# A state-space scan that steps over pairs of time steps, with its lookup tables built as products of two small ones

## The reference, cut to what matters

```
mag = exp(a_re * dt); lb = mag * (cos(a_im * dt) + i sin(a_im * dt))
bb = coef * b                                 # per group 64 x 16, complex
bu[l, g, p] = sum_c u[l, g, c] * bb[g, p, c]
x[l] = lb * x[l-1] + bu[l]                    # along all 512 tokens
y[l, g, c] = Re(sum_p c[g, c, p] * x[l, g, p]) + d_skip[g, c] * u[l, g, c]
s = gelu(y); s = s * sigmoid(s @ w_glu + b_glu)
y_b = (s * silu(ssm_gate)) @ w_ssm_out
```

## Time and profile before

| | |
|---|---|
| time, median of 3 runs (lowest, highest) | 1187.76 us (1187.38, 1188.01) |
| the profiled execution: its own time | 1186.81 us |
| the profiled execution: span, first to last instruction | 1185.0 us |
| mean granted clock of PE, of full speed | 0.998 |
| busy: PE, weight loads of PE, DVE, ACT, POOL | 1158.0, 949.8, 752.5, 403.4, 11.8 us |

### The profile page before, as it was taken

How to read it: one execution, slowest core, us unless ns; L and a number is a source line. 1 busy time by engine, 2 the same in 40 slices (tenths; PEclk the granted TensorE clock), 3 DMA queues, 4 the chain that set the end, 5 groups by cost and what they waited for, 6 DMA issues and landing times.

```text
span 1185.0 us, 13271 instructions
## 1 busy us (share of the span) xinstructions
PE 1158.0 (98%) x5357; PEld 949.8 (80%) x5357; DVE 752.5 (64%) x1317; ACT 403.4 (34%) x526; POOL 11.8 (1%) x12
## 2 busy tenths in 40 slices
PE   5999999999999999999999999999999999999997
PEld 4999888888777788887777777788888888887886
DVE  5887568999777778628999999443133343423324
ACT  7423243332376543332222323233222223313114
POOL 3000000000000000000000000000000000000000
PEclk9999999999999999999999999999999999999999
DMA  7444323223332237443433443332443343245223
GB/s 248 107 107 108 106 72 101 77 76 103 98 115 90 72 98 216 131 137 110 139 107 107 137 130 90 106 103 76 107 107 87 92 107 104 77 169 219 78 101 142
DMA packets 171885, 134.86 MB, mean 114 GB/s; under 512 B 10968, under 2 KB 158768, under 8 KB 170672
## 3 DMA queue, kind: packets, MB, share of 16 engines
q1 hardware_dynamic: 162912, 124.73, 36.1%
q10 hardware_dynamic: 8912, 9.29, 2.2%
HBM read 121.42 MB, written 12.58 MB: 113 GB/s over the span
## 4 chain that ended last, share of the span: by engine, by line
PE 83%; DVE 13%; DMA 1%; ACT 1%; issue 1%; SPq 0%; DVEq 0%; ACTq 0%
PE bank L405 21%; PE bank L407 20%; PE bank L406 20%; PE bank L655 5%; PE bank L657 5%; PE bank L656 5%; DVE w_lo L992 3%; DVE score L1097 2%; DVE small L1096 2%; PE bank L557 1%; PE bank L597 1%; PE bank L538 1%; DVE score L1085 1%; DMA xt<-in_x 1%; PE bank L547 1%
## 5 line engine op out<-in xcount | busy, mean ns | idle before, releaser
L405 PE MATMUL bank<-act_hi,w_hi 128*128 128x512 f32 (+1 forms) x1088 | 422.5, 388 | 2.6 <-DVE w_lo L992 2.6
L406 PE MATMUL bank<-act_lo,w_hi 128*128 128x512 f32 (+1 forms) x1088 | 416.9, 383 | 0.0
L407 PE MATMUL bank<-act_hi,w_lo 128*128 128x512 f32 (+1 forms) x1088 | 416.9, 383 | 0.0
L992 DVE TENSOR_TENSOR w_lo<-w_raw,w_hi 128x2048 fp32r<-128x2048 f32 x96 | 219.6, 2288 | 177.9 <-ACT w_hi L703 177.0
L703 ACT ACTIVATE w_hi<-w_raw 128x2048 fp32r<-128x2048 f32 (+1 forms) x97 | 184.8, 1905 | 184.1 <-DMA w_raw<-in_w_out 104.9
L405 PEld LDWEIGHTS bank<-act_hi,w_hi 128*128 128x128 f32 x1088 | 204.4, 188 | 48.5 <-issue 9.6
L407 PEld LDWEIGHTS bank<-act_hi,w_lo 128*128 128x128 f32 x1088 | 204.3, 188 | 38.5
L406 PEld LDWEIGHTS bank<-act_lo,w_hi 128*128 128x128 f32 x1088 | 204.5, 188 | 34.7
L655 PE MATMUL bank<-w_hi,act_hi 128*128 128x512 f32 x192 | 74.7, 389 | 0.0
L656 PE MATMUL bank<-w_lo,act_hi 128*128 128x512 f32 x192 | 74.7, 389 | 0.0
L657 PE MATMUL bank<-w_hi,act_lo 128*128 128x512 f32 x192 | 74.7, 389 | 0.0
(11 more groups left out here) (249 smaller groups left out, 1300.9 us busy)
## 6 DMA issues: line engine op xcount, KB each, us to landing
w_raw<-in_w_in SPq DMA_DIRECT2D x68, 1024.0 KB, 5.6
w_raw<-in_w_out SPq DMA_DIRECT2D x16, 1024.0 KB, 5.5
e_tables<-e_made ACTq DMA_DIRECT2D x16, 512.0 KB, 2.9
w_raw<-in_w_att_out SPq DMA_DIRECT2D x8, 1024.0 KB, 5.9
e_tab<-e_tables SPq DMA_DIRECT2D x16, 512.0 KB, 6.5
xt<-in_x SPq DMA_DIRECT2D x4, 1024.0 KB, 8.1
w_raw<-in_w_ssm_out SPq DMA_DIRECT2D x4, 1024.0 KB, 5.0
res<-in_x SPq DMA_DIRECT2D x4, 1024.0 KB, 11.7
```

Of the source, the lines that this page charges most:

```text
L405: nc.tensor.matmul(out_ap, wh, x_hi[k], start=(j == 0), stop=False)
L406: nc.tensor.matmul(out_ap, wh, x_lo[k], start=False, stop=False)
L407: last = nc.tensor.matmul(out_ap, wl, x_hi[k], start=False, stop=(j == n - 1))
L992: v.tensor_tensor(w_lo[:, u % SLOTS, :], w_raw[:, u % SLOTS, :], w_hi[:, u % SLOTS, :].bitcast(F32), ALU.subtract).then_inc(split_done, 1)
```

## The change

The scan runs over pairs of time steps, so it has 256 steps instead of 512, with the squared factor MAG * MAG.

- u is written with its even and odd tokens apart. For each tile T of two pairs (8 tiles) SP turns u by four DMAs so that a row is a channel and a parity (`turn_u`), and the products with b for both parities are one matmul of 64 rows and 256 columns, for each of the two pairs and for real and imaginary part (`bu_of`). These are float32 matmuls and not split ones.
- y of odd tokens comes from the state, y of even ones from the state before it with c * lb (`c_lam`) and a direct term: a block matrix `direct` (c by b, and d_skip on its diagonal) by u, one float32 matmul of 128 x 128 by 256 columns for each tile. ACT copies y out and turns it back by four DMAs (`y_out`).
- The tables are not stored and loaded. `e_fine` holds 16 fine and 16 coarse rotations of each pair, and DVE makes a tile's table as their product (`make_e`, 6 instructions for two pairs). `e_base`, `e_point`, `e_whole`, `store_e` and `load_e` are gone.
- In attout the b and c preparation stands ahead of `low_through(attout 2)`, PE transposes c after attout 2, multiplies c by b and transposes b after attout 4.
- gelu(3) follows the tile of ssmgate unit 2, not of unit 1.

```
# SP
+            def turn_u(T):
+                i, a = T // 2, T % 2
+                if T >= 2:
+                    sp.wait_ge(bu_done, T - 1)
+                else:
                     sp.wait_ge(tile_done, TILE0["merge0"])
+                for b in range(2):
+                    for par_ in range(2):
+                        sp.dma_start(u_turn[64 * b + 32 * par_:64 * b + 32 * par_ + 32, T % 2, :],
+                                     uT[64 * a + 32 * b:64 * a + 32 * b + 32, i, par_ * HALVES:(par_ + 1) * HALVES]
+                                     ).then_inc(u_moved[T % 2], 16)
...
                 if n == 2:
-                    load_e(0)
-                    load_e(1)
-                if 4 <= n < PAIRS + 2:
-                    load_e(n - 2)
+                    turn_u(0)
+                    turn_u(1)
+                if n >= 4 and n % 2 == 0 and n // 2 < TILES:
+                    turn_u(n // 2)
# PE
+            for i in range(3):
                 attout(u0 + i, i)
             pe.wait_ge(ssm_w_ready, 1)
             for r in range(2):
                 for q in range(QUADS):
+                    last = nc.tensor.transpose(sum_bank[r][:, q * P:(q + 1) * P], c_nat[:, r, q, :], ident[:, :])
             last.then_inc(ssm_w_turned, 1)
+            for i in (3, 4):
                 attout(u0 + i, i)
+            pe.wait_ge(c_w_done, 1)
+            for q in range(QUADS):
                 for r in range(2):
+                    last = nc.tensor.matmul(sum_bank[0][:, q * P:(q + 1) * P], b_own[:, r, 4 * q:4 * q + 4, :, :],
+                                            c_w[:, r, 4 * q:4 * q + 4, :], start=(r == 0), stop=(r == 1))
+            last.then_inc(cb_done, 1)
+            for r in range(2):
+                for T in range(TILES):
+                    last = nc.tensor.transpose((pair_bank, turn_bank)[r][T // 4][:, T % 4 * P:(T % 4 + 1) * P],
+                                               b_blk[:, r, 2 * T:2 * T + 2, :, :, :], ident[:, :])
+            last.then_inc(ssm_w_turned, 1)
+            for i in (5, 6, 7):
+                attout(u0 + i, i)
+            def bu_of(T):
...
+                pe.wait_ge(u_moved[T % 2], 64 * (T // 2 + 1))
+                into = [bank[:, :] for bank in (pair_bank, turn_bank)[T % 2]]
+                for r, b in ((0, 0), (0, 1), (1, 0), (1, 1)):
+                    rows = slice(64 * b, 64 * b + 64)
+                    last = nc.tensor.matmul(into[b][:, r * HALVES:(r + 1) * HALVES], b_w[rows, r, T, :], u_turn[rows, T % 2, :],
+                                            start=True, stop=True)
+                    last.then_inc(bu_part, 1)
+                nc.tensor.matmul(sum_bank[T % 2][:, 0:HALVES], direct[:, T, :], u_turn[:, T % 2, :], start=True, stop=False
+                                 ).then_inc(bu_done, 1)
+            def y_of(T):
+                pe.wait_ge(x_ready, T + 1)
                 for r in range(2):
+                    for b in range(2):
+                        for par_ in range(2):
+                            cols_ = slice(64 * b + 32 * par_, 64 * b + 32 * par_ + 32)
+                            last = nc.tensor.matmul(sum_bank[T % 2][cols_, 0:HALVES], (c_lam, c_w)[par_][:, r, 2 * T + b, :],
+                                                    x_ri[:, r, b, par_:par_ + HALVES], start=False, stop=(r == 1))
...
+                if n % 2 == 1 and n // 2 < TILES:
+                    bu_of(n // 2)
+                if n % 2 == 1 and 1 <= n // 2 <= TILES:
+                    y_of(n // 2 - 1)
+                project(name, h_hi, h_lo, KD)(UNIT0[name] + i, i)
# ACT, in ssmgate
                 t = TILE0["ssmgate"] + i
-                copy_tile(t, gate_s[:, i, :], stream_bank[t % 2][:, :], ACT.Silu)
                 if i == 1:
+                    y_out(TILES - 1)
+                copy_tile(t, gate_s[:, i, :].rearrange("p (s k) -> p k s", s=2), stream_bank[t % 2][:, :].rearrange("p (k s) -> p k s", s=2),
+                          ACT.Silu)
+                if i == 2:
                     gelu(QUADS - 1)
                 high_through(UNIT0["ssmgate"] + i + 2)
# DVE, in attout
             low_through(UNIT0["u"] + 5)
-            e_whole(E_EARLY)
-            e_whole(E_EARLY + 1)
-            for i in (0, 1, 2):
-                low_through(UNIT0["attout"] + i + 2)
-                e_whole(E_EARLY + 2 * i + 2)
-                e_whole(E_EARLY + 2 * i + 3)
             dve.wait_ge(bc_loaded, 9 * 16)
             for r, op in ((0, ALU.subtract), (1, ALU.add)):
                 tt(b_bar[:, r, :, :], b_raw[:, r, :, :], spread(p_(CR), GCH), ALU.mult)
                 tt(t_b, b_raw[:, 1 - r, :, :], spread(p_(CI), GCH), ALU.mult)
                 tt(b_bar[:, r, :, :], b_bar[:, r, :, :], t_b, op)
+            for r, op in ((0, ALU.subtract), (1, ALU.add)):
+                tt(b_lam[:, r, :, :], b_bar[:, r, :, :], spread(p_(LBR), GCH), ALU.mult)
+                tt(t_b, b_bar[:, 1 - r, :, :], spread(p_(LBI), GCH), ALU.mult)
+                tt(b_lam[:, r, :, :], b_lam[:, r, :, :], t_b, op)
             for r in range(2):
+                for par_, b_ in ((0, b_lam), (1, b_bar)):
+                    for g in range(2):
+                        link(v.tensor_scalar(b_blk[:, r, :, par_, g, :], b_[:, r, :, :], cols[:, 2 + g:3 + g], None, ALU.mult))
+                link(v.tensor_copy(b_own[:, r, :, :, :], b_blk[:, r, :, 1, :, :]))
+            low_through(UNIT0["attout"] + 2)
# DVE, in merge0, for each tile T, with n = 2 * T + 1
+                dve.wait_ge(bu_part, 4 * T + 4)
...
+                merge_gate(n - 1)
...
+                low_through(UNIT0["merge0"] + n + 1)
...
+                if T + 1 < TILES:
+                    made = make_e(T + 1)
+                low_through(UNIT0["merge0"] + n + 2)
+                merge_gate(n)
+            dve.wait_ge(y_done, 4 * TILES)
...
+            low_through(UNIT0["ssmgate"] + 2)
             for k in range(QUADS):
                 dve.wait_ge(gelu_done, k + 1)
                 split_s(k, s_ready)
```

More of the change, by code:

```diff
@@ L585, in _ @@
                 attout(u0 + i, i)
[L588 to L593, removed]
-                for r in range(2):
[L595 to L613, removed]
-                for r in range(2):
[L615 to L622, removed]
+            pe.wait_ge(c_w_done, 1)
@@ L880, in _ @@
                                          ).then_inc(c_w_done, 1)
+                if i == 10:
+                    act.wait_ge(cb_done, 1)
+                    act.wait_ge(direct_ready, 1)
+                    for jj in range(4):
+                        a, b = jj // 2, jj % 2
+                        here, there = slice(32 * jj, 32 * jj + 32), slice(64 * b, 64 * b + 32)
+                        nc.scalar.activation(direct[there, a:TILES:2, there],
+                                             sum_bank[0][here, :].rearrange("p (q n) -> p q n", q=QUADS)[:, :, here], ACT.Copy
+                                             ).then_inc(cb_copied, 1)
@@ L889, in _ @@
             act.wait_ge(tile_done, TILE0["merge0"])
-            u_high_part(0)
+            for r in range(2):
+                last = nc.scalar.activation(b_w[:, r, 0:4, :].rearrange("p t n -> p (t n)"), (pair_bank, turn_bank)[r][0][:, :], ACT.Copy)
+            last.then_inc(b_w_done, 1)
+            act.wait_ge(direct_ready, 2)
             for j in range(KD):
@@ L893, in _ @@
                 high_through(UNIT0["merge0"] + j + 2)
+                if j % 2 == 1 and j >= 3:
+                    y_out(j // 2 - 1)
                 if j >= 2:
@@ new lines, in _ @@
+            low_through(UNIT0["attout"] + 4)
+            dve.wait_ge(c_w_done, 1)
+            for r, op in ((0, ALU.add), (1, ALU.subtract)):
+                tt(c_lam[:, r, :, :], c_w[:, r, :, :], spread(p_(LBR), 2 * GCH), ALU.mult)
+                tt(spare[:, :, :], c_w[:, 1 - r, :, :], spread(p_(LBI), 2 * GCH), ALU.mult)
+                tt(c_lam[:, r, :, :], c_lam[:, r, :, :], spare[:, :, :], op)
+            low_through(UNIT0["attout"] + 6)
+            dve.wait_ge(cb_done, 1)
+            v.memset(direct[:, :, :], 0.0).then_inc(direct_ready, 1)
@@ new lines, in _, with mark @@
+            low_through(UNIT0["attout"] + 7)
+            dve.wait_ge(cb_copied, 4)
+            for T in range(TILES):
+                last = v.scalar_tensor_tensor(direct[:, T, :], ident[:, :], small[:, D_COL + T:D_COL + T + 1], direct[:, T, :], ALU.mult, ALU.add)
+            last.then_inc(direct_ready, 1)
+            def mark(ins):
+                count[0] += 1
+                ins.then_inc(v_step, 1)
+                return count[0]
+            p0, p1, p2, p3 = (prod[:, i, :] for i in range(4))
@@ new lines, in _ @@
+            last.then_inc(b_w_done, 1)
+            link(v.memset(x_ri[:, :, :, 0:1], 0.0))
+            made = make_e(0)
+            low_through(UNIT0["merge0"] + 2)
+            for T in range(TILES):
+                n = 2 * T + 1
```

(18 more changed lines are left out.)

300 lines of the change are left out of this document (122 added, 178 removed).

## The result

The changed kernel takes 1192.28 us (median of 6 runs, 1192.21 to 1193.72), the kernel before, measured beside it, 1187.81 (6 runs, 1187.38 to 1188.17): ratio 1.004, 95% interval 1.0027 to 1.0052. The profiled execution took 1192.25 with a span of 1190.5, which is 5.5 more than the span before, and 5.5 was the sum. Part of that agreement is luck. The profiled execution before was 1.0 under its median, so the medians are only 4.5 apart. And the terms were off and cancelled: merge0 came out 0.9 better than taken, the clock 0.5 and attention 0.4, the opening, counted at next to nothing, 1.6 worse, and the wait at ssmgate 3 0.3 worse.

What follows compares the result with a forecast made beforehand. PE was taken as the bound, busy 1158.0 of 1185.0 us. Terms -6.6 + 2.9 + 2.1 + 6.2 + 2.0 - 1.2 + 0.1 = +5.5 put the profiled 1186.81 at 1192.3, median 1193.3, range 1186 to 1201.

Steps and rivals of the forecast that it cites:

- Part 1: merge0's small matmuls on PE: 3.1 us against 3.93 per pair of pairs, a gain of 6.6 for eight.
- Part 2: attout: more transposes, eight float32 matmuls and two stream breaks on PE, nothing hiding them, +2.9 us.
- Part 3: attout 2: PE waits 2.1 us for a low part behind DVE's DMA wait and b and c preparation.
- Part 4: ssmgate 3: PE idles 6.2 us for a low part behind the later gelu(3), plus 2.0 for the clock.
- The clock's 2.0: Behind the wait at ssmgate 3: PE's clock falls in the gap, and coming back costs 2.0 us.
- Part 5: Work DVE and ACT are rid of: attention waits -1.2 us, merge0 slack worth nothing; a copy in the opening +0.1.
- The small tiles that overlap no better than before: Rival, merge0: y_of stays at 1.84, +5.1, 1198.4; with bu_of one after another too, 1205; chance 0.18.
- The wait that doesn't come: Rival, ssmgate 3: no wait there, so 6.2 + 2.0 go and the time is 1185.1, faster; chance 0.10.
- Turned data that is late: Rival, merge0: a tile's small DMAs or y's way back come late, 1 us each gives 1201; chance 0.08.
- DVE as the hidden bound of merge0: Rival, merge0: DVE was the hidden bound and its relief shows, inside part 1's bounds; chance 0.02.

Runs made afterwards that it cites:

- Two cures of it, from either end: Each against the changed kernel: ssmgate's fourth unit's low part before DVE's wait for the last Gelu, 1184.06; last Gelu ahead of ACT's third ssmgate tile, 1183.35.

## Why the prediction was right, point by point

**Part 1, merge0: right in sign, short by about 1 us.** 3.1 per pair of pairs was taken, 24.72 - 21.76 = 2.96 came. From attout's end to the start of ssmgate 3, less the wait, the gain is 7.5 (before 763.00 - 524.88 = 238.12; after 766.84 - 529.77 - 6.47 = 230.60), against 6.6. bu_of was 1.06 for 0.95, y_of 1.00 for 1.2: four at once and not something between two and four. Direct, with what surrounds it, was 0.63 for 0.445, and the changes of shape taken at 0.50 were what is left, 2.96 - 2.69 = 0.27. Here the sum held better than its terms.

**Part 2, attout: right.** Attout takes 529.77 - 436.00 = 93.77 us, before 524.88 - 435.92 = 88.96. Less the wait of 1.97, 2.84 is more work, against 2.9.

**Part 3, the wait at attout 2: right,** 1.97 for 2.1, through the step that it named: from 448.01 DVE needs 9.56 us to the low part, against 9.5. Moving that low part took the wait away and 1.8 us.

**Part 4, the wait at ssmgate 3: right,** 6.47 for 6.2. The chain was worked out with a Silu of 0.60; it took 1.05 to 1.10 because of how gate_s is now written. With the plain write the wait is 6.02, 0.2 under the forecast, so two small errors of opposite sign are in this term. Two cures of it, from either end, gave 8.2 and 8.9. The clock's 2.0 was 1.5 in the profile shown. It isn't one number: in the seven profiles of kernels that keep the wait of 6.0 to 6.5 us, the unit behind it took 12.39, 12.49, 12.56, 13.60, 13.62, 13.89 and 13.90, so the clock cost 1.5 to 3.0, mean 2.3.

**Part 5: attention right in cause and short in size, the opening wrong.** Attention's waits fell by 1.2, as taken, but the stretch to attout became 1.57 shorter, and 1.80 in the kernel before without e_point. In merge0 DVE's relief gave nothing, and no wait came; DVE was busy for 17.0 us of a tile's 24.72 and not 18.8. But "one short copy on DVE in the opening: +0.1, at most 0.4" failed. Attout starts at 436.00, with all that shorter, where it was 435.92: the opening took 1.65 back. Part of it starts in ACT's timeline at the very beginning, the kernel before and then the changed one:

```profile
3.32 0.26 ACTq L715 DMA_DIRECT2D row_tile<-in_ssm_d  x1
3.61 0.37 ACTq L716 DMA_DIRECT2D small<-in_log_dt  x1
...
5.80 1.91 ACT L723 ACTIVATE square<-xt 128x2048 f32<-128x2048 f32 x1 [0.30 <-DMA xt<-in_x]
```

```profile
3.27 1.58 ACTq L722 DMA_DIRECT2D row_tile<-in_ssm_d  x2
4.89 0.47 ACTq L724 DMA_DIRECT2D small<-in_log_dt  x1
...
6.91 1.91 ACT L731 ACTIVATE square<-xt 128x2048 f32<-128x2048 f32 x1
```

d_skip is brought in by these lines, where one transfer in the list of `row_tile` did it before:

```
+            for par_ in range(2):
+                act.dma_start(row_tile[100:108, :].rearrange("t (b s c) -> t b s c", b=2, s=2)[:, :, par_, :],
+                              d_skip[0].rearrange("(t b g) c -> t b (g c)", t=TILES, b=2)).then_inc(rows_loaded, 16)
```

Issuing them holds ACT for 1.58 us and not 0.26; the first Square of the RMS norm starts at 6.91 and not 5.80, and PE's first transposes at 10.91 and not 9.80. But at most half of that delay lasts. PE's timeline shows where the rest comes in, the kernel before and then the changed one (for its earlier rows see the earlier trace rows):

```profile
36.73 0.34 PE L405 MATMUL bank<-act_hi,w_hi 128*128 128x384 f32 x1
```

```profile
21.18 0.78 PE L471 MATMUL banks<-act_hi,w_hi 128*80 128x512 f32 x1
...
26.01 0.48 PE L471 MATMUL banks<-act_hi,w_hi 128*80 128x512 f32 x1
...
38.38 0.34 PE L407 MATMUL banks<-act_hi,w_hi 128*128 128x384 f32 x1
```

The first matmul by weights is 0.53 late (21.18, before 20.65), the first unit behind it 1.65 (38.38, before 36.73). In between PE's matmuls went on at half rate up to about 26.0, before up to about 22.8. In the twelve profiles of the changed kernel and its variants PE starts at 10.90 to 11.14, the first matmul by weights comes at 20.55 to 21.18, and the first unit behind it starts at 37.07 to 38.41; in the two of the old order these are 9.80 and 9.92, 20.65 and 20.75, 36.73 and 37.09. So PE's early waits swallow at least half of the 1.1 us. What is left of the 1.65 is the clock's return, for in neither profile has PE a wait behind that first matmul; and the start of that unit differs by 1.3 us among executions whose opening has the same code. Whether it comes later because PE starts later is open: no run undid the two transfers alone.

**The rivals.** The small tiles that overlap no better than before: not so. The wait that doesn't come: it came. Turned data that is late: no wait of PE or of the Gelu shows it. DVE as the hidden bound of merge0: 26 us more on it changed nothing.

## What to carry to other kernels

When work is moved or added on an engine that works through a hand-written list, look at what stands behind it in the list and who needs that: 88 us less on DVE gained nothing in merge0, and two low parts of 2.3 us behind the wrong waits cost 10. Put what PE needs next ahead of a wait for anything else. Count the issue time of every small transfer on an engine that also computes, and then follow the delay: here 1.1 us at PE's start was at most 0.5 some ten us later. And compare profiles stage by stage before an end-to-end difference is put down to an edit, because an opening with the same code differed by over 1 us.

## What the hardware showed that was not expected

- Float32 matmuls into different groups of 32 output rows run side by side even when the next but one writes the same group again: eight take 1.00 and 1.01 us in the two orders, 3.58 in one group.
- An ACT activation of 128 x 512 that writes its output alternately into two halves takes 1.10 us, straight 0.60. The copies into yb, whose writes go two elements apart, take 0.63.
- After a gap of 6.5 us, PE's clock was back at 2.4 GHz in the profile of the changed kernel some 3 us after work began again, and in that of the version with doubled tables some 6 us after. At the opening the first matmul at full rate was at 26.01 in the changed kernel and at 23.80 in the version with bu_of reordered, with attout's start at 436.00 and 434.65. So one profile's term for the clock is uncertain by about 1.5 us with the code there unchanged.
